# Writing each block's gates to DRAM in eight transfers of 512 KB, one beside each slab of the next block, in place of one transfer of 4 MB

## The reference

```python
experts = e1 * N_KEYS + e2                        # e1, e2 in 0..127
gates = jax.nn.softmax(sv, axis=-1)
a = jnp.einsum('cd,ced->ce', h_c, u[e_c])         # token with its experts' u rows
act = jax.nn.gelu(a, approximate=False) * g_c
out = jnp.einsum('ce,ced->cd', act, v[e_c])
```

## Time and profile before

| | us |
|---|---|
| median of three runs | 2816.53 |
| the three runs | 2816.53, 2813.70, 2821.87 |
| profiled execution | 2818.3 |
| its span | 2816.5 |
| PE busy | 2587.7 (92%) |
| POOL busy | 1792.3 (64%) |
| DVE busy | 1667.6 (59%) |
| ACT busy | 727.3 (26%) |

### The profile page before, as it was taken

The page is one execution under the profiler, slowest core; times in us unless marked ns, Lnnn a source line. Parts: engine busy times, 40 slices in busy tenths (PEclk is TensorE's granted clock), DMA queues, the critical chain, the costliest instruction groups (busy, mean ns, idle before and its releaser), DMA issues.

```text
span 2816.5 us, 36632 instructions
## 1 busy us (share of the span) xinstructions
PE 2587.7 (92%) x12764; PEld 2166.2 (77%) x12764; DVE 1667.6 (59%) x3128; ACT 727.3 (26%) x1296; POOL 1792.3 (64%) x1315
## 2 busy tenths in 40 slices
PE   4989799999899998999989989999889999999998
PEld 2866578888586675677778889899889977777777
DVE  5447532111343325453459998778778387887888
ACT  4158320000222323433210011111112133323232
POOL 2746557767551243375646568888887688878775
PEclk8989899999998998999999999999999999999999
DMA  6224222222220021122222337887887699989996
GB/s 238 90 88 144 90 75 105 90 104 91 94 75 15 31 75 34 46 105 75 75 97 107 113 139 277 334 327 294 328 326 268 258 338 333 332 312 334 324 323 235
DMA packets 154451, 502.82 MB, mean 179 GB/s; under 512 B 11616, under 2 KB 78816, under 8 KB 122080
## 3 DMA queue, kind: packets, MB, share of 16 engines
q1 hardware_dynamic: 96432, 311.98, 31.4%
q0 software_dynamic: 36864, 134.23, 12.5%
q10 hardware_dynamic: 21040, 55.11, 5.1%
HBM read 448.84 MB, written 52.43 MB: 178 GB/s over the span
## 4 chain that ended last, share of the span: by engine, by line
PE 60%; DVE 13%; POOL 9%; DMA 9%; issue 4%; ACT 3%; SPq 0%; ACTq 0%; DVEq 0%; POOLq 0%
PE banks L545 8%; PE banks L547 8%; PE banks L546 8%; POOL W_lo L407 6%; DMA arena<-gates_dram 4%; PE banks L905 3%; PE banks L906 3%; PE banks L907 3%; PE banks L675 3%; PE banks L820 2%; PE banks L821 2%; PE banks L822 2%; DMA B_lo_plain<-u_rows,arena 2%; PE banks L693 2%; POOL W_hi L415 2%
## 5 line engine op out<-in xcount | busy, mean ns | idle before, releaser
L407 POOL TENSOR_TENSOR W_lo<-raw,W_hi 128x2048 fp32r<-128x2048 f32 x127 | 585.5, 4611 | 62.8 <-ACT W_hi L1319 57.4
L432 POOL TENSOR_TENSOR W_lo<-raw,W_hi 128x512 fp32r<-128x512 f32 x376 | 493.6, 1323 | 0.0
L435 POOL TENSOR_TENSOR beat<-zero 128x1 f32<-128x1 f32 x94 | 19.1, 204 | 651.0 <-PE banks L695 255.9
L820 PE MATMUL banks<-A_hi,W_hi 128*128 128x384 f32 x1024 | 383.0, 374 | 11.9 <-ACT B_plain L1257 9.8
L822 PE MATMUL banks<-A_hi,W_lo 128*128 128x384 f32 x1024 | 347.5, 339 | 0.0
L821 PE MATMUL banks<-A_lo,W_hi 128*128 128x384 f32 x1024 | 347.4, 339 | 0.0
L905 PE MATMUL banks<-W_hi,B_hi 128*128 128x512 f32 x768 | 305.6, 398 | 30.6 <-DVE B_lo L1828 30.6
L906 PE MATMUL banks<-W_hi,B_lo 128*128 128x512 f32 x768 | 303.9, 396 | 0.0
L907 PE MATMUL banks<-W_lo,B_hi 128*128 128x512 f32 x768 | 303.4, 395 | 0.0
L545 PE MATMUL banks<-A_hi,W_hi 128*128 128x512 f32 x680 | 265.9, 391 | 4.9 <-issue 4.9
L547 PE MATMUL banks<-A_hi,W_lo 128*128 128x512 f32 x680 | 264.9, 389 | 0.0
(11 more groups left out here) (259 smaller groups left out, 5514.0 us busy)
## 6 DMA issues: line engine op xcount, KB each, us to landing
raw<-weights SPq DMA_DIRECT2D x241, 1024.0 KB, 4.8
gelu_dram<-B_plain ACTq DMA_DIRECT2D x64, 384.0 KB, 6.4
gates_dram<-arena ACTq DMA_DIRECT2D x6, 4096.0 KB, 20.2
arena<-gelu_dram SPq DMA_DIRECT2D x64, 384.0 KB, 7.0
arena<-gates_dram SPq DMA_DIRECT2D x64, 384.0 KB, 10.3
W_plain<-weights SPq DMA_DIRECT2D x4, 1024.0 KB, 16.1
X<-x_t SPq DMA_DIRECT2D x1, 2048.0 KB, 14.6
arena<-v_rows,arena POOLq DMA_INDIRECT x128, 8.4
```

What stands on the lines that cost most here:

```text
L407: pool.tensor_tensor(W_lo[:, s % 2, :], raw[:, s % 2, :], W_hi[:, s % 2, :].bitcast(F32), ALU.subtract)\
L432: return pool.tensor_tensor(W_lo[:, j, cols], raw[:, j, cols], W_hi[:, j, cols].bitcast(F32), ALU.subtract)
L820: mm(to, lh, rh, start=k == 0, stop=False)
```

## The change

Each block's gates are written in eight transfers of 512 KB (16 of the 128 first keys in each, 4 KB in one piece per partition). The transfers of block q go out during block q+1, one behind the gelu write of each of its 8 slabs; in the last block, which has only 4 slabs with tokens, two behind each. The last block's own eight go out in two groups of four, ahead of the two slabs that follow. The counts of `g_stored` are changed to fit. ACT's loop over pairs of slabs is written out, so that its program has no registers and branches there; what the loop computes stays the same.

```diff
+STORES = 8
...
-                    sp.wait_ge(g_stored[j], 8 * GB)
-                    sp.wait_ge(g_stored[1 - j], 8 * GB)
+                    sp.wait_ge(g_stored[j], 8 * STORES * GB)
+                    sp.wait_ge(g_stored[1 - j], 8 * STORES * GB)
...
-                pool.wait_ge(g_stored[i], 8 * GB)
+                pool.wait_ge(g_stored[i], 8 * STORES * GB)
...
+            def store_gates(q, part):
+
+                if part == 0:
+                    act.wait_ge(g_copied, 8 + GT * (q + 1))
+                e = KEYS // STORES
+                act.dma_start(g_dram[q][:, e * part:e * part + e, :].rearrange("p e t -> p (e t)"),
+                              g_stage[:, q % 2, GT * e * part:GT * e * part + GT * e])\
+                    .then_inc(g_stored[q % 2], 16)
...
-                    act.wait_ge(g_stored[q % 2], 16 * (q // 2))
+                    act.wait_ge(g_stored[q % 2], 16 * STORES * (q // 2))
...
-                act.wait_ge(g_copied, 8 + GT * (q + 1))
-                act.dma_start(g_dram[q].rearrange("p e t -> p (e t)"), g_stage[:, q % 2, :])\
-                    .then_inc(g_stored[q % 2], 16)
-                for s in range(first + with_tokens, first + with_tokens + between):
-                    gelus(s)
+                for s in range(with_tokens):
+                    gelus(first + s, tokens=lambda j: tokens(2 * s + j))
+                    if q:
+                        per_slab = STORES // with_tokens
+                        for part in range(per_slab * s, per_slab * s + per_slab):
+                            store_gates(q - 1, part)
+                for s in range(between):
+                    for part in range(STORES // 2 * s, STORES // 2 * (s + 1) if s < 2 else 0):
+                        store_gates(q, part)
+                    gelus(first + with_tokens + s)
```

More of the change, by code:

```diff
@@ L1286, in _, with tokens @@
                 if q >= 2:
-                    act.wait_ge(g_stored[q % 2], 16 * (q // 2))
+                    act.wait_ge(g_stored[q % 2], 16 * STORES * (q // 2))
                 stage = g_stage[:, q % 2, :].rearrange("p (e t) -> p e t", t=GT)
                 per_half = GT // (2 * with_tokens)
[L1290 to L1303, removed]
-                act.wait_ge(g_copied, 8 + GT * (q + 1))
-                act.dma_start(g_dram[q].rearrange("p e t -> p (e t)"), g_stage[:, q % 2, :])\
-                    .then_inc(g_stored[q % 2], 16)
-                for s in range(first + with_tokens, first + with_tokens + between):
-                    gelus(s)
+                def tokens(half):
+                    for i in range(per_half // 4):
+                        j = per_half * half + 4 * i
+                        act.wait_ge(hot_used, GT * q + j + 8)
+                        act.activation(stage[:, :, j:j + 4],
+                                       bank[4 + j // 4 % 2][:, :].rearrange("p (t e) -> p e t", t=4), ACT.Copy)\
+                            .then_inc(g_copied, 4)
+                for s in range(with_tokens):
[8 more added lines that the diff above has]
+                    gelus(first + with_tokens + s)
                 first += with_tokens + between
```

## The result

| | before | changed | ratio, 95% interval |
|---|---|---|---|
| first comparison, medians of 5 and 5 runs | 2816.53 | 2795.59 | 0.9914 (0.9896 to 0.9931) |
| second, of 17 and 6 runs | 2819.43 | 2801.66 | 0.9936 (0.9924 to 0.9949) |
| third, of 11 and 6 runs | 2820.03 | 2798.17 | 0.9927 (0.9904 to 0.9949) |

The change is faster by 0.6 to 0.9%, some 18 to 22 us by the medians. The forecast was 2785 us, a gain of 31.6.

What follows compares the result with a forecast made beforehand. PE bounds the kernel, stopped once a block by gathers late beside the 4 MB gates' write; POOL limits next. Terms 32.1 - 1.0 - 0.5 + 1.0 = 31.6 us give 2785 us, likeliest 2780 to 2790, range 2776 to 2801.

Steps and rivals of the forecast that it cites:

- late in part: Rival: gathers over 9.4 us hold POOL too in every slab of blocks 2 to 5; gain 15.6 us, 2801 us; chance 0.15.
- What held PE before: u stage: each block's 4 MB gates' write delays gathers, so PE waits four times for DVE's one-hots, 28.6 us in all.
- POOL as the next limit: Gathers' stretch: without waits POOL takes 386.4 us for 37 slabs instead of 415.0, so it can be done 28.6 us sooner.
- PE's distance to POOL: How far PE must stay behind POOL's split for first gathers to land: 0.5 to 1.75 us, taken as 1.0, paid once.
- PE's earlier start: PE starting right at the last split's end, not at 2141.7: 32.1 us gained, where POOL is done 28.6 us sooner.
- ACT's added wait: First gates' copy of blocks 3 to 6 waits for a write just issued: 0.5 us in all, 0 to 6 kept.
- The last two writes: Writes of blocks 5 and 6: splitting the former gains nothing, the latter 1.0 us, as a slab's load isn't late.
- The v stage: Stage after the u stage: same data from the same places, only begins sooner; nothing counted.
- given back in the v stage: Rival: the v stage ends when it did, so time stays within 0.3%, 2813 us; chance 0.06.
- A write costs more than its bytes: Rival: from 2.8 us engine time per write, not 1.25, no gain; at 3.1, 10 us slower, 2827 us; chance 0.06.
- the second estimate of this rival: From the Trainium skill's fixed 2.0 us per DMA: a write costs 3.25 us, a slab 11.75 instead of 11.3, 14 us slower.
- PE's limit, not POOL's: Rival: POOL's gaps shrink or PE uses its lead longer; gain up to 39.8 + 1.0 us, 2776 us; chance 0.05.

## Why the prediction came out as it did

*The number.* The first comparison's 2795.59 us lie in the stated range of 2776 to 2801, but not in the 2780 to 2790 that the prediction gave its own mechanism. It was inside by the room that was made for a rival, "late in part", which was not what happened. The mechanism was right, and two thirds of the forecast gain came.

*What held PE before* was as told. The four stops for DVE are gone once the write is spread, and stay when only the loop is changed.

*POOL as the next limit* was right, and so was its size: 386.0 us between the two splits against 386.4, once nothing else held it. With POOL relieved, PE was busy without a gap for 170 us. One sign that was named for it did not come: no wait of PE for `W_lo` stands in the tables of the change. That POOL is the limit is read from its own beat and from the version that relieves it.

*PE's distance to POOL*, put at 1.0 us once, can't be read from a row by itself. The stage without ACT's wait is 543.0 (mean of two) less 513.1 (mean of the two versions), 29.9 us shorter; the sum without its ACT term was 32.1. The terms were thus too high by some 2 us together. Between the two splits POOL gave 29.4 us (415.3 less 385.9, means of two), where 28.6 was forecast. What the sum added to that, 3.5 us for PE's earlier start and 1.0 for the last write less 1.0 of distance, gave only some 0.5. The engines' share was put at 94% and is 98%, and the gathers land after 9.2 us, above the 8.2 that 6.9 + 1.25 would have made. The small waits for DVE that are left, 3.8 us, fit this.

*ACT's added wait* is the term that was mis-sized: 0.5 us was taken, 0 to 6 kept. It costs 520.3 (mean of three) less 513.1, 7.2 us, more than the 6 that was kept for it. The path is seen in POOL's waits for PE between the splits: 6.9, 4.4 and 6.9 us in the three profiles of the change, none above 0.5 us in the two versions with an earlier last write. Of the third profile's, 1.4 us come from a stop for DVE, so the 7.2 are a little too high. The landing was put together as 6.5 us of a gelu's write plus 1.25. But those 6.5 come from a stretch with the engines at 84%, and now the write itself fills them. It took 10.5 us in the median, and the row above shows 11.7 (1873.01 to 1884.75), where 7.6 was the limit; 1.61 of them went into issuing it, for which 0.5 was taken. PE waiting for ACT's gelu at the blocks' starts was one of the prediction's own signs of being wrong, and it came. The step "such a stall comes out of PE's distance" failed too: POOL stood 3.7 us behind the first stop. The likely reason is that gathers of 9 us had already taken part of the 3.7 us of distance; this is argued and not measured. The clock at the lower of its levels for some microseconds behind a stop (mean 0.91 from 1880 to 1900, and 0.68 from 1885.7 to 1891) adds to it.

*The last two writes*: the 1.0 us counted for them is not shown. PE's wait of 1.04 us behind the sixth is gone, but it was 0.2 us in the second profile of the kernel before and is absent with one write of 4 MB and the loop written out. From the second split to the stage's end are 103.9 and 101.5 us before, 101.7 in that version, and 102.7, 102.1 and 103.3 in the change. There ACT issues the last two writes of the fifth block and four of the sixth in a row, and a gelu is held until they are out, for which PE waits 0.5 us, the fourth of its waits for ACT:

```profile
2179.58 6.41 ACTq L1290 DMA_DIRECT2D gates_dram<-arena  x6
```

*The v stage*, put at no change, can't be settled within 4 us. The two profiles of the kernel before have 581.0 and 585.6, the three changed ones 586.5, 581.7 and 586.5, and versions of either kind lie between 579.3 and 587.9. So it spreads by some 5 us for one and the same kernel, and whether the change adds 1 or 2 us to it is open. That much would account for the medians' gain, 18 to 22 us, being less than the stage's 22.7. The rival "given back in the v stage" would have needed some 20 us more there, which is excluded.

*The rivals.* "Still late in part" gave 2801 for a reason that was not the one at work: the gathers' lateness cost little, and ACT's wait most. "A write costs more than its bytes" did not happen: a write took 1.27 us of engine time in the change, by its pieces, where 1.25 was the sum's term, 2.8 the point of no gain, and 3.25 the second estimate of this rival. With 16 partitions, at 2.5 to 2.6 us, the gain between the splits shrank from 22 to 7 us, which is its mechanism short of the point of no gain. What made that version slower than before is ACT's issuing behind the last block, which no rival had. "PE's limit, not POOL's" did not happen in the change; it took the high part off POOL to come near it.

## What to carry to other kernels

A large write that nobody waits for can still stop the core, by what it makes late; spread it over the work that has spare DMA time, in pieces across all partitions, and count what issuing several in a row costs the engine that issues them. When a transfer is spread until just before its buffer is needed, the wait for it becomes a wait on its last piece: leave that piece at least one step of room, and size its landing with the engines as full as the change makes them. Look next at the limit right behind the one removed: here POOL's 10.44 us a slab against PE's 10.14, worth another 5 us.

## What was not expected of the hardware

A write of 512 KB from 16 partitions took 2.5 to 2.6 us of engine time, and from 128 partitions 1.2 to 1.3 us, with pieces of 32 KB as with pieces of 4. The DMA engines at 99% busy and 358 GB/s did not hold PE back at all, for 170 us. And issuing a transfer from ACT took 0.55 us for a gelu, and for an eighth of the gates from 0.5 to 1.9 us in the change. In a row, eight of them took from 4.9 to 8.5 us, and six of those from 16 partitions 18.9.
